# First norm of a two-block transformer step on one core: rows turned unscaled, root applied at copy-out, table loads moved

## Chip, core and metric

The kernel runs on one core of one Trainium2 chip, as one program. The metric is the device time of one execution in microseconds (us). TensorE is called PE in rows of the profile, VectorE DVE, ScalarE ACT, GpSimd POOL, and SyncE SP (it only issues DMAs). SPq and ACTq are the DMA-issuing instructions of SyncE and ScalarE.

## What is computed

Two blocks follow each other on x, 256 tokens of 2048 values, all in fp32. Only the first stage of the first block matters here:

```python
xn = rms_norm(h, pre_mix_norm[i])   # x * rsqrt(mean(x*x) + eps) * gain
proj = xn @ w_in[i]                 # 2048 x 4608
```

Then come head norms with rotary angles on the first heads (gains `q_norm`, `k_norm`), a neighbourhood attention with a relative position bias and a global attention, `w_o`, an MLP, a gate, and the second block with its own projections, conv, scan and MLP. Nine further norms and all other weights are untouched by the change.

The root is one number per token, the gain one number per channel. With r a token's root, (r x g) W = r ((x g) W): the root can be applied to the product's rows.

## The kernel before

**Tiling.** Tokens lie on partitions in two halves (TH = 2 of 128). Each weight matrix is streamed once, in pieces of 512 KB: 256 rows (two times 128, `raw[:, slot, 2, 512]`) by 512 columns. Eight pieces are a chunk of 512 output columns; w_in has nine chunks, pieces 0 to 71. NSLOT = 4 pieces are held.

**Split arithmetic.** A piece lands in `raw` (SyncE, `load`, L507). ScalarE writes `whi`, its value in the matmul's reduced format (`split`, L595); VectorE writes the remainder `wlo = raw - whi` (L1492). TensorE multiplies hi by hi, hi by lo and lo by hi for both token halves and both 128-row blocks, 12 matmuls of 128x512 a piece (L1075), into two PSUM banks per chunk, pairs of banks in turn. The stationary side is `xhi` and `xlo`, the transposed activations, in 16 blocks kt of 128 channels.

**What orders the stream.** Piece p is loaded when `lo_done` has reached p - 3, so when its slot's `raw` has been split. ScalarE splits piece p when it has landed and TensorE has finished piece p - 4. TensorE's `chunk` waits for `lo_done`. ScalarE and VectorE run three pieces ahead of TensorE in program order: in `chunk(p)`, step u splits piece p + 3 + u, and what stands in `extra` goes ahead of that split. A chunk's copy-out (`evac_to`, L611) comes after its eight steps.

**The norm.** `norm("norm0")` on ScalarE squares token half 0 (L619) and VectorE half 1 (L1507); VectorE forms the mean (L1510), GpSimd the power -0.5 (L2004), and then each scales one half into `xs` (L621, L1515). TensorE turns `xs` in eight groups of four 128x128 transposes into two PSUM banks in turn (`turn`, L1050); ScalarE copies a group out with the gain as `xhi` (L626), VectorE makes `xlo` (L1521). `first_chunk` puts groups 0 to 3 before piece 0 and groups 4 to 7 between pieces 0, 1 and 2.

**What is loaded at the start.** SyncE's queue: the identity (`small`), fifteen loads of small vectors as rows of 128 values into `vecs` (L499), the rope tables and column mask (`early`, L501), then the weight pieces. ScalarE's queue: x (`res`, L636), the bias table copied 64 times within memory (`bias_rows`, L637), and `gqk`, where q_norm (512 bytes) is copied to 128 partitions times 8 heads (L638) and k_norm to 128 times 2 (L640). TensorE turns all vectors into columns in one go (L1100) and VectorE copies them into `cols` (L1540); norm0's gain and 15 others lie there. The columns of c_2 get an exp at the start (L645) and the rest of their silu only before `postnorm("post0")`.

**Bias.** `bias_load` (L524) gathers 32 loads of 64 KB from `bias_rows` into `bm`, two after each piece of chunks 1 and 2. When all are in, GpSimd adds the column mask to `bm` in one instruction (L2015), and only then serves the head rotations that VectorE starts with chunk 4's splits.

Of the kernel before, what the change touches and what calls it, by code (L numbers as in the profile page):

```python
# [7 lines left out]
ALU = mybir.AluOpType  # L8
# [6 lines left out]
P = 128  # L15
T = 256
# [24 lines left out]
    [("pre_mix_norm", 16), ("pre_mlp_norm", 16), ("pre_ple_norm", 16), ("norm_pre_mix_2", 16),  # L41
# [74 lines left out]
def build(nc, I, out):  # L116

    ctx = ExitStack()
    with ctx:
# [64 lines left out]
        vecs = at("vecs", [P, len(VEC_GROUPS), P], F32, work_at + 48 * K)  # L184
# [97 lines left out]
        x_in = sem("x_in")  # L282
# [203 lines left out]
        def _(sp):  # L486
            sp.dma_start(small[:], I["k_small"]).then_inc(small_in, 16)
            for gi, group in enumerate(VEC_GROUPS):
                r = 0
                for name, rows in group:  # L490
                    if name == "conv_dw_w_2a":
                        src = I["conv_dw_w_2"][0].rearrange("a (b p) -> (a b) p", p=P)[0:128]
                    elif name == "conv_dw_w_2b":
                        src = I["conv_dw_w_2"][0].rearrange("a (b p) -> (a b) p", p=P)[128:248]
                    elif name == "c_ctx_2":
                        src = I[name].rearrange("(b p) -> b p", p=P)
                    else:
                        src = I[name][0].rearrange("(b p) -> b p", p=P)
                    sp.dma_start(vecs[r:r + rows, gi, :], src).then_inc(vec_in, 16)  # L499
                    r += rows  # L500
            sp.dma_start(early[:], I["k_early"]).then_inc(early_in, 16)  # L501
# [85 lines left out]
        def _(act):  # L587
# [42 lines left out]
            def postnorm(k, row, wait_row, gain):  # L630
# [5 lines left out]
            act.dma_start(res[:], rows_of(I["x"][0])).then_inc(x_in, 16)  # L636
            act.dma_start(bias_rows, bass.AP(I["rel_pos_bias"].tensor, 0, [[0, GRID], [1, NB]])).then_inc(bias_copied, 16)  # L637
            act.dma_start(gqk[:, 0:A_Q * HD].rearrange("p (h d) -> p h d", d=HD),  # L638
                          bass.AP(I["q_norm"].tensor, 0, [[0, P], [0, A_Q], [1, HD]])).then_inc(gqk_in, 16)
            act.dma_start(gqk[:, A_Q * HD:].rearrange("p (h d) -> p h d", d=HD),  # L640
                          bass.AP(I["k_norm"].tensor, 0, [[0, P], [0, A_KV], [1, HD]])).then_inc(gqk_in, 16)
            for u in range(3):
                split(u, u)
            act.wait_ge(vec_cols, 1)
            nc.scalar.activation(stat[:, 64:96], cols[:, COL["c_2"]:COL["c_2"] + 32], ACT.Exp, scale=-1.0).then_inc(c_exp, 1)  # L645
            norm("norm0", res, lambda e: e.wait_ge(x_in, 16), col("pre_mix_norm"))
            p0, g0 = plan["in"]
            with act.Fori(0, 4) as i:
                for c in range(2):
                    chunk(i * 16 + (8 * c + p0), evac_to(proj, i * (2 * NCH) + c * NCH, g0 + c))  # L650
            chunk(p0 + 64, evac_to(proj, 8 * NCH, g0 + 8))
# [392 lines left out]
        def _(pe):  # L1044
# [50 lines left out]
            pe.wait_ge(small_in, 16)  # L1095
            pe.wait_ge(vec_in, 16 * sum(len(g) for g in VEC_GROUPS))
            c = 0
            for gi, group in enumerate(VEC_GROUPS):
                rows = sum(n for _, n in group)
                ins = nc.tensor.transpose(ps[:, MB, c:c + rows], vecs[0:rows, gi, :], ident[0:rows, 0:rows])  # L1100
                c += rows
            ins.then_inc(vec_turned, 1)

            p0, g0 = plan["in"]
            pe.wait_ge(S["xs", "norm0"], 2)
            first_chunk(p0, g0, lambda n: norm_turn("norm0", n), 8, t_free, TG["norm0"][0])
            with pe.Fori(0, 4) as i:
                for c in (1, 2):
                    chunk(i * 16 + (8 * c + p0), i * 2 + (g0 + c), xhi, xlo, par=g0 + c)
# [368 lines left out]
        def _(dve):  # L1478
# [58 lines left out]
            for u in range(3):  # L1537
                split(u, u)
            dve.wait_ge(vec_turned, 1)
            nc.vector.tensor_copy(cols[:], ps[:, MB]).then_inc(vec_cols, 1)  # L1540
            norm("norm0", res, lambda e: e.wait_ge(x_in, 16), col("pre_mix_norm"))
# [45 lines left out]
            for c in range(IN1 // NCH):  # L1587
                chunk(p0 + 8 * c, extra=rotate(c - 4) if 4 <= c < 8 else {})
# [46 lines left out]
            dve.wait_ge(c_exp, 1)  # L1635
            cc, ce = cols[:, COL["c_2"]:COL["c_2"] + 32], stat[:, 64:96]
            step(nc.vector.tensor_scalar(ce, ce, 1.0, None, ALU.add))
            step(nc.vector.reciprocal(ce, ce))
            nc.vector.tensor_tensor(ce, ce, cc, ALU.mult).then_inc(silu_done, 1)
            dve.wait_ge(silu_done, 1)  # L1640

# [473 lines left out]
```

## Time and profile before

| | us |
|---|---|
| median of 3 runs | 3124.39 (3123.58 to 3125.54) |
| profiled execution, its own time | 3127.27 |
| its span in the trace | 3125.5 |
| PE busy | 2863.6 (92%) |
| DVE busy | 2080.2 (67%) |
| ACT busy | 1338.3 (43%) |
| POOL busy | 210.7 (7%) |

The profiled execution lies 2.9 us above the median. A busy share is a mean over stages with different limits. "Idle before" in a row, in square brackets, is how long the engine stood before the instruction and what ended it. PEclk is the granted TensorE clock, 1.00 being 2.4 GHz. The DMA share is that of 16 engines. Matmuls are pipelined and their ends modelled, so that rows of neighbours overlap.

### The profile page before, as it was taken

What the parts mean: (1) busy time and instruction counts of PE and PEld (TensorE: products, weight loads), DVE (VectorE), ACT (ScalarE), POOL (GpSimd) and SP (SyncE); (2) the same over time, 40 slices, a digit from 0 to 9 for tenths busy, and PEclk for the clock granted to TensorE, in tenths of its full rate; (3) what the DMA queues carried; (4) which work ended last, traced back from release to release, by engine and by line L of the source; (5) the groups of instructions that cost most, each with busy time, mean ns of one, the idle gap of its engine ahead of it and who ended that gap; (6) DMA issues with size and microseconds to landing.
All of it is one profiled execution on the core that took longest, in us unless ns stands there. A gap on an engine that the chain in (4) does not pass through costs nothing.

```text
span 3125.5 us, 39386 instructions
## 1 busy us (share of the span) xinstructions
PE 2863.6 (92%) x13257; PEld 2376.2 (76%) x13257; DVE 2080.2 (67%) x2265; ACT 1338.3 (43%) x1571; POOL 210.7 (7%) x116
## 2 busy tenths in 40 slices
PE   4998959999999996959799999999996999999997
PEld 3786848878888885747578888888875888888886
DVE  3565479889897986577658549566646555555555
ACT  3346434344343434433444444564443434344443
POOL 0100011010010101030000000000001101010000
PEclk9999979999999998979899999999997999999998
DMA  6761648888888883645266666512653666666664
GB/s 168 197 195 55 194 149 292 304 289 292 277 296 293 296 299 123 199 148 162 87 219 197 198 186 195 168 55 74 210 188 108 208 213 206 220 199 217 207 207 150
DMA packets 322563, 620.29 MB, mean 198 GB/s; under 512 B 27399, under 2 KB 29575, under 8 KB 320647
## 3 DMA queue, kind: packets, MB, share of 16 engines
q1 hardware_dynamic: 318439, 597.93, 60.4%
q10 hardware_dynamic: 3936, 19.96, 2.0%
q8 instruction: 105, 1.72, 0.2%
q14 instruction: 83, 0.68, 0.1%
HBM read 613.62 MB, written 5.15 MB: 198 GB/s over the span
## 4 chain that ended last, share of the span: by engine, by line
PE 85%; DVE 7%; DMA 2%; issue 2%; ACT 2%; SPq 1%; POOL 1%; DVEq 0%; ACTq 0%; POOLq 0%
PE ps L1075 79%; DMA raw<-w_in 2%; DVE wlo L1492 1%; PE ps L1050 1%; PE ps L1186 1%; PE ps L1196 1%; DVE res L1535 1%; DVE tcol L1739 1%; DVE xs L1532 1%; PE ps L1378 1%; PE ps L1396 1%; PE ps L1358 1%; DVE xlo L1731 0%; POOL res L2008 0%; DVE lg L1772 0%
## 5 line engine op out<-in xcount | busy, mean ns | idle before, releaser
L1492 DVE TENSOR_TENSOR wlo<-raw,whi 128x1024 fp32r<-128x1024 f32 x943 | 1173.4, 1251 | 840.0 <-ACT whi L595 835.8
L595 ACT ACTIVATE whi<-raw 128x1024 fp32r<-128x1024 f32 x943 | 998.6, 1061 | 1378.5 <-PE ps L1075 1260.2
L1075 PE MATMUL ps<-whi,xhi 128*128 128x512 f32 x2656 | 1050.0, 395 | 38.2 <-DVE wlo L1492 20.3
L1075 PE MATMUL ps<-wlo,xhi 128*128 128x512 f32 x2656 | 1041.1, 392 | 0.0
L1075 PE MATMUL ps<-whi,xlo 128*128 128x512 f32 x2656 | 1041.1, 392 | 0.0
L1075 PEld LDWEIGHTS ps<-whi,xhi 128*128 128x128 f32 x2656 | 503.8, 190 | 148.4 <-issue 31.2
L1075 PEld LDWEIGHTS ps<-whi,xlo 128*128 128x128 f32 x2656 | 503.2, 189 | 106.4
L1075 PEld LDWEIGHTS ps<-wlo,xhi 128*128 128x128 f32 x2656 | 504.0, 190 | 102.7
L1075 PE MATMUL ps<-whi,hhi 128*128 128x512 f32 x1040 | 406.7, 391 | 0.0
L1075 PE MATMUL ps<-whi,hlo 128*128 128x512 f32 x1040 | 404.7, 389 | 0.0
L1075 PE MATMUL ps<-wlo,hhi 128*128 128x512 f32 x1040 | 404.6, 389 | 0.0
L1662 DVE SCALAR_TENSOR_TENSOR macc<-mraw,stat,macc 128x512 f32<-128x512 f32 x480 | 354.0, 767 | 4.5
L1075 PEld LDWEIGHTS ps<-whi,hlo 128*128 128x128 f32 x1040 | 195.2, 188 | 40.8
L1075 PEld LDWEIGHTS ps<-whi,hhi 128*128 128x128 f32 x1040 | 195.3, 188 | 39.7
L1075 PEld LDWEIGHTS ps<-wlo,hhi 128*128 128x128 f32 x1040 | 195.3, 188 | 39.6
L2036 POOL TENSOR_TENSOR sqrow<-rrow 128x512 f32<-128x512 f32 x64 | 106.4, 1683 | 1226.9 <-ACT rrow L726 1226.9
L1050 PE MATMUL ps<-small,xs 128*128 128x128 f32 x192 | 39.7, 370 | 138.0 <-ACT xs L759 38.9
L1050 PEld LDWEIGHTS ps<-small,xs 128*128 128x128 f32 x192 | 30.6, 190 | 146.6 <-ACT xs L759 39.5
L726 ACT ACTIVATE rrow<-ps 128x512 f32<-128x512 f32 x64 | 34.8, 596 | 65.0 <-PE ps L1075 65.0
L1679 DVE TENSOR_TENSOR yrow<-ps,yrow 128x512 f32<-128x512 f32 x64 | 41.2, 686 | 25.3 <-PE ps L1075 25.3
L2004 POOL TENSOR_TENSOR stat<-stat 128x2 f32<-128x2 f32 x11 | 7.8, 705 | 743.5 <-DVE stat L1510 743.5
L1819 DVE SCALAR_TENSOR_TENSOR yT<-uT,cols,yT 128x252 f32<-128x252 f32 (+17 forms) x144 | 52.9, 432 | 0.0
(238 smaller groups left out, 1628.2 us busy)
## 6 DMA issues: line engine op xcount, KB each, us to landing
raw<-w_in SPq DMA_DIRECT2D x296, 512.0 KB, 4.3
raw<-mlp_w SPq DMA_DIRECT2D x259, 512.0 KB, 4.4
mraw<-w_mod SPq DMA_DIRECT2D x192, 512.0 KB, 5.4
raw<-w_up SPq DMA_DIRECT2D x128, 512.0 KB, 5.3
raw<-w_down SPq DMA_DIRECT2D x128, 512.0 KB, 5.3
raw<-w_o SPq DMA_DIRECT2D x32, 512.0 KB, 4.5
raw<-w_ple_gate SPq DMA_DIRECT2D x32, 512.0 KB, 4.6
raw<-w_out SPq DMA_DIRECT2D x32, 512.0 KB, 4.6
```

Of the source, the lines that this page charges most:

```text
L595: nc.scalar.activation(whi[:, s % NSLOT], raw[:, s % NSLOT], ACT.Copy).then_inc(hi_done, 1)
L726: ins = nc.scalar.activation(rrow[:, th], ps[:, bank(g0 + j) + th], ACT.Relu)
L1050: ins = nc.tensor.transpose(ps[:, TB[t % 2], c:c + P], src, ident)
L1075: ins = nc.tensor.matmul(ps[:, bank(par) + th], a[:, kt, th * P:(th + 1) * P], b[:, (s + u) % NSLOT, k], start=(kt == 0 and m == 0), stop= ...
L1186: ins = nc.tensor.transpose(ps[:, TB[(t0 + h) % 2], a * T + th * P:a * T + (th + 1) * P], sqrow[:, th, f:f + P], ident)
L1196: ins = nc.tensor.matmul(ps[:, MB, bass.ds(n * 8 + (2 * b + v), 1)], macc[:, v, m % 3, b * P:(b + 1) * P], ones[:, 0:1], start=True, stop= ...
L1358: ins = nc.tensor.matmul(out_of[:, :, 0:4:3] if d == 0 else out_of[:, :, 1:3], w, sums_r[:, m:m + 2].rearrange("p l (r c) -> p l r c", r=2 ...
L1492: nc.vector.tensor_tensor(wlo[:, s % NSLOT], raw[:, s % NSLOT], whi[:, s % NSLOT].bitcast(F32), ALU.subtract)\
L1662: ins = nc.vector.scalar_tensor_tensor(out=a, in0=w, scalar=x, in1=a, op0=ALU.mult, op1=ALU.add)
L1679: ins = nc.vector.tensor_tensor(y, ps[:, bank(g0 + j) + th], y, ALU.add)
L1819: nc.vector.scalar_tensor_tensor(out=y, in0=tap_part(uT[:, ct], ct, dd, True), scalar=wcol(TAPS // 2 + dd, ct), in1=y, op0=ALU.mult, op1=A ...
L2036: nc.gpsimd.tensor_tensor(sqrow[:, th], rrow[:, th], rrow[:, th], ALU.mult).then_inc(sq_done, 1)
```

## The change

- The gain of norm0 is loaded alone, first after the identity, turned and copied to `cols` alone.
- x is loaded in two halves of the channels, with a semaphore each. TensorE turns `res` itself (`x_turn`), groups 0 and 1 before piece 0, group u + 2 ahead of piece u. The copy-outs with the gain (`x_high`, `x_low`) stand between the splits. Nothing is scaled before the product.
- The square sums of x and the mean are computed ahead of the split of piece 9, into scratch (`xjunk`). The copy-out of each of w_in's nine chunks applies the root, as a per-partition scale (`evac_scaled`); ScalarE's loop over chunks is written out.
- The fourteen other vector loads go out after piece 4, their transposes stand before piece 10 and their copy in chunk 1. `early`, `bias_rows` and both `gqk` loads go out after piece 8, all on SyncE's queue. The bias gathers follow the pieces of chunks 2 and 3.
- The silu of the c columns is finished in chunk 3 instead of ahead of post0.

The diff, cut to its core:

```diff
@@ SyncE
+            sp.dma_start(vecs[0:KT, 0, :], I["pre_mix_norm"][0].rearrange("(b p) -> b p", p=P)).then_inc(gain_in, 16)
+            def vector_loads():
+                for gi, group in enumerate(VEC_GROUPS):
...
+            def attention_loads():
+                sp.dma_start(early[:], I["k_early"]).then_inc(early_in, 16)
+                sp.dma_start(bias_rows, bass.AP(I["rel_pos_bias"].tensor, 0, [[0, GRID], [1, NB]])).then_inc(bias_copied, 16)
+                sp.dma_start(gqk[:, 0:A_Q * HD].rearrange("p (h d) -> p h d", d=HD),
+                             bass.AP(I["q_norm"].tensor, 0, [[0, P], [0, A_Q], [1, HD]])).then_inc(gqk_in, 16)
+                sp.dma_start(gqk[:, A_Q * HD:].rearrange("p (h d) -> p h d", d=HD),
+                             bass.AP(I["k_norm"].tensor, 0, [[0, P], [0, A_KV], [1, HD]])).then_inc(gqk_in, 16)
-            chunk(w_in, 0, 0)
-            for c in (1, 2):
-                chunk(w_in, 8 * c, c * NCH, extra={u: (lambda n=16 * (c - 1) + 2 * u: two_biases(n)) for u in range(8)})
-            with sp.Fori(3, IN1 // NCH) as i:
+            chunk(w_in, 0, 0, extra={4: vector_loads})
+            chunk(w_in, 8, NCH, extra={0: attention_loads})
+            for c in (2, 3):
+                chunk(w_in, 8 * c, c * NCH, extra={u: (lambda n=16 * (c - 2) + 2 * u: two_biases(n)) for u in range(8)})
+            with sp.Fori(4, IN1 // NCH) as i:
@@ ScalarE
+            for h in range(2):
+                act.dma_start(res[:, :, h * (D // 2):(h + 1) * (D // 2)],
+                              rows_of(I["x"][0])[:, :, h * (D // 2):(h + 1) * (D // 2)]).then_inc(x_in[h], 16)
+            def x_high(g):
+                t0 = TG["norm0"][0]
+                act.wait_ge(t_done, t0 + g + 1)
+                for j in range(2):
+                    kt = 2 * g + j
+                    ins = nc.scalar.activation(xhi[:, kt], ps[:, TB[(t0 + g) % 2], j * T:(j + 1) * T], ACT.Copy, scale=gain0[:, kt:kt + 1])
+                ins.then_inc(t_hi, 1)
...
+            def evac_scaled(dst, col, g, k):
+                def f():
+                    act.wait_ge(rstd_done, RMS[k] + 1)
+                    for th in range(TH):
+                        ins = nc.scalar.activation(dst[:, th, bass.ds(col, NCH)], ps[:, bank(g) + th], ACT.Copy,
+                                                   scale=stat[:, 8 + th:9 + th])
+                    ins.then_inc(acc_free, 1)
+                return f
+            act.wait_ge(vec_cols, 1)
+            split(0, 0)
+            x_high(0)
+            x_high(1)
+            split(1, 1)
+            x_high(2)
+            split(2, 2)
+            for c in range(IN1 // NCH):
+                chunk(p0 + 8 * c, evac_scaled(proj, c * NCH, g0 + c, "norm0"),
+                      extra={0: {1: lambda: x_high(3), 2: lambda: x_high(4), 3: lambda: x_high(5), 4: lambda: x_high(6),
+                                 5: lambda: x_high(7), 6: x_square}, 2: {0: c_exps}}.get(c, {}))
@@ TensorE
+            def x_turn(g):
+                pe.wait_ge(x_in[g // 4], 16)
+                turn(TG["norm0"][0] + g, [(j * T + th * P, res[:, th, (2 * g + j) * P:(2 * g + j + 1) * P])
+                                          for j in range(2) for th in range(TH)])
+            def x_part(u):
+                if u + 2 < 8:
+                    x_turn(u + 2)
+                pe.wait_ge(t_free, TG["norm0"][0] + u + 1)
+            def other_vectors():
+                pe.wait_ge(vec_in, 16 * sum(len(g) for g in VEC_GROUPS[1:]))
+                pe.wait_ge(vec_cols, 1)
+                turn_vectors(1, len(VEC_GROUPS))
-            pe.wait_ge(S["xs", "norm0"], 2)
-            first_chunk(p0, g0, lambda n: norm_turn("norm0", n), 8, t_free, TG["norm0"][0])
+            turn_vectors(0, 1)
+            x_turn(0)
+            x_turn(1)
+            chunk(p0, g0, xhi, xlo, inserts={u: (lambda u=u: x_part(u)) for u in range(8)})
+            chunk(p0 + 8, g0 + 1, xhi, xlo, inserts={2: other_vectors})
+            chunk(p0 + 16, g0 + 2, xhi, xlo)
@@ VectorE
+            def x_mean_square():
...
+            nc.vector.tensor_copy(cols[:, 0:KT], ps[:, MB, 0:KT]).then_inc(vec_cols, 1)
+            split(0, 0)
+            x_low(0)
+            x_low(1)
+            split(1, 1)
+            x_low(2)
+            split(2, 2)
+            in_extra = {0: {1: lambda: x_low(3), 2: lambda: x_low(4), 3: lambda: x_low(5), 4: lambda: x_low(6), 5: lambda: x_low(7),
+                            6: x_mean_square}, 1: {4: other_columns}, 3: {1: silu_columns}}
```

## Rows read from the trace of the kernel before

**Rows 1.** The page: its span and the chain that ended last, by engine.
```profile
span 3125.5 us, 39386 instructions
...
PE 85%; DVE 7%; DMA 2%; issue 2%; ACT 2%; SPq 1%; POOL 1%; DVEq 0%; ACTq 0%; POOLq 0%
```

**Rows 2.** Timeline of the start: start us, us, engine, line, operation, out<-in, count, [idle before].
```profile
1.24 0.60 ACTq L637 DMA_DIRECT2D bias_rows<-rel_pos_bias  x1
...
2.50 3.06 ACTq L640 DMA_DIRECT2D gqk<-k_norm  x1
...
8.04 0.29 SPq L499 DMA_DIRECT2D vecs<-conv_ln_b  x1
...
24.39 1.27 PE L1100 MATMUL ps<-small,vecs 112*128 112x112 f32 x5 [24.39 <-DMA vecs<-conv_ln_b]
...
28.95 1.06 ACT L595 ACTIVATE whi<-raw 128x1024 fp32r<-128x1024 f32 x1 [22.08 <-DMA raw<-w_in]
...
30.04 3.79 DVE L1492 TENSOR_TENSOR wlo<-raw,whi 128x1024 fp32r<-128x1024 f32 x3 [30.04 <-ACT whi L595]
...
37.73 2.00 ACT L621 ACTIVATE xs<-res,stat 128x2048 f32<-128x2048 f32 x1 [1.15 <-POOL stat L2004]
...
39.79 1.97 PE L1050 MATMUL ps<-small,xs 128*128 128x128 f32 x8 [14.13 <-ACT xs L621]
...
40.94 1.69 ACT L626 ACTIVATE xhi<-ps,cols 128x256 fp32r<-128x256 f32 x4 [1.21 <-PE ps L1050]
...
41.82 1.73 DVE L1521 SCALAR_TENSOR_TENSOR xlo<-ps,cols,xhi 128x256 fp32r<-128x256 f32 x4 [2.80 <-ACT xhi L626]
...
44.43 0.78 PE L1075 MATMUL ps<-whi,xhi 128*128 128x512 f32 x1
...
48.85 1.03 PE L1050 MATMUL ps<-small,xs 128*128 128x128 f32 x8
```

**Rows 3.** DMA issues of the whole execution: issuer, count, size, median us to landing.
```profile
raw<-w_in SPq DMA_DIRECT2D x296, 512.0 KB, 4.3
...
res<-x ACTq DMA_DIRECT2D x1, 2048.0 KB, 8.4
...
bias_rows<-rel_pos_bias ACTq DMA_DIRECT2D x1, 930.0 KB, 10.1
...
gqk<-k_norm ACTq DMA_DIRECT2D x1, 128.0 KB, 25.1
```

**Rows 4.** Windows: start:end, length, busy by engine, PEclk, DMA share, GB/s.
```profile
18.00:19.00 1.00, 0.00 (x0) 0.00 (x0) 0.00 (x0) 0.00 (x0) 0.00 (x0) 1.00 0.88 33
...
27.00:28.00 1.00, 0.00 (x0) 0.00 (x0) 0.00 (x0) 0.00 (x0) 0.00 (x0) 1.00 1.06 409
```

**Rows 5.** DMA queue of ScalarE, 11.3 to 25 us: packets, MB, share of 16 engines.
```profile
q10 hardware_dynamic: 1046, 0.53, 81.9%
```

**Rows 6.** Timeline of ScalarE, copy-outs of chunks 0, 3 and 4.
```profile
71.07 1.09 ACT L611 ACTIVATE proj<-ps 128x512 f32 x2 [0.82 <-PE ps L1075]
...
144.54 1.09 ACT L611 ACTIVATE proj<-ps 128x512 f32 x2 [1.75 <-PE ps L1075]
...
166.30 1.09 ACT L611 ACTIVATE proj<-ps 128x512 f32 x2 [1.75 <-PE ps L1075]
```

**Rows 7.** Timeline of TensorE, first matmuls after two later waits.
```profile
1568.39 0.47 PE L1075 MATMUL ps<-whi,xhi 128*128 128x512 f32 x1 [2.98 <-DVE wlo L1492]
...
2376.92 0.79 PE L1075 MATMUL ps<-whi,xhi 128*128 128x512 f32 x1 [3.95 <-DVE xlo L1731]
```

**Rows 8.** Timeline around the mask addition on GpSimd.
```profile
106.64 8.96 POOL L2015 TENSOR_TENSOR bm<-bm,early 128x4096 f32<-128x4096 f32 x1 [68.94 <-DMA bm<-bias_rows]
...
106.88 13.20 DVE L1492 TENSOR_TENSOR wlo<-raw,whi 128x1024 fp32r<-128x1024 f32 x4 [1.26 <-ACT whi L595]
...
116.73 0.80 PE L1075 MATMUL ps<-whi,xhi 128*128 128x512 f32 x1 [4.99 <-DVE wlo L1492]
```

**Rows 9.** The window behind the wait at 116.73, columns as in rows 4.
```profile
118.00:120.00 2.00, 2.00 (x6) 1.52 (x6) 2.00 (x2) 0.00 (x0) 0.00 (x0) 0.50 0.88 262
```

More of the change, by code:

```diff
@@ L501, in _ @@
-            sp.dma_start(early[:], I["k_early"]).then_inc(early_in, 16)
+            sp.dma_start(vecs[0:KT, 0, :], I["pre_mix_norm"][0].rearrange("(b p) -> b p", p=P)).then_inc(gain_in, 16)
+            def vector_loads():
+                for gi, group in enumerate(VEC_GROUPS):
+                    r = 0
+                    for name, rows in group if gi else ():
+                        if name == "conv_dw_w_2a":
+                            src = I["conv_dw_w_2"][0].rearrange("a (b p) -> (a b) p", p=P)[0:128]
+                        elif name == "conv_dw_w_2b":
+                            src = I["conv_dw_w_2"][0].rearrange("a (b p) -> (a b) p", p=P)[128:248]
+                        elif name == "c_ctx_2":
+                            src = I[name].rearrange("(b p) -> b p", p=P)
+                        else:
+                            src = I[name][0].rearrange("(b p) -> b p", p=P)
+                        sp.dma_start(vecs[r:r + rows, gi, :], src).then_inc(vec_in, 16)
+                        r += rows
@@ L647, in _ @@
[L647 to L651, printed above, removed]
+            for h in range(2):
+                act.dma_start(res[:, :, h * (D // 2):(h + 1) * (D // 2)],
+                              rows_of(I["x"][0])[:, :, h * (D // 2):(h + 1) * (D // 2)]).then_inc(x_in[h], 16)
+            gain0 = col("pre_mix_norm")
@@ L1092, in first_chunk, with turn_vectors @@
                 chunk(p, g, xhi, xlo, inserts={u: (lambda u=u: before(u)) for u in range(8)})
-            pe.wait_ge(small_in, 16)
[L1096 to L1104, printed above, removed]
-            pe.wait_ge(S["xs", "norm0"], 2)
-            first_chunk(p0, g0, lambda n: norm_turn("norm0", n), 8, t_free, TG["norm0"][0])
-            with pe.Fori(0, 4) as i:
-                for c in (1, 2):
+            def turn_vectors(first, last):
+                c = sum(n for group in VEC_GROUPS[:first] for _, n in group)
+                for gi, group in enumerate(VEC_GROUPS[first:last], first):
+                    rows = sum(n for _, n in group)
+                    ins = nc.tensor.transpose(ps[:, MB, c:c + rows], vecs[0:rows, gi, :], ident[0:rows, 0:rows])
+                    c += rows
+                ins.then_inc(vec_turned, 1)
+            def x_turn(g):
[10 more added lines that the diff above has]
+                turn_vectors(1, len(VEC_GROUPS))
+            p0, g0 = plan["in"]
+            pe.wait_ge(small_in, 16)
+            pe.wait_ge(gain_in, 16)
+            turn_vectors(0, 1)
[4 more added lines that the diff above has]
+            chunk(p0 + 16, g0 + 2, xhi, xlo)
+            with pe.Fori(0, 3) as i:
+                for c in (3, 4):
                     chunk(i * 16 + (8 * c + p0), i * 2 + (g0 + c), xhi, xlo, par=g0 + c)
@@ L1535, in postnorm, with x_low @@
                 nc.vector.tensor_tensor(res[:, 1], res[:, 1], xs[:, 1], ALU.add).then_inc(S["res", k], 1)
-            for u in range(3):
-                split(u, u)
-            dve.wait_ge(vec_turned, 1)
-            nc.vector.tensor_copy(cols[:], ps[:, MB]).then_inc(vec_cols, 1)
-            norm("norm0", res, lambda e: e.wait_ge(x_in, 16), col("pre_mix_norm"))
+            gain0, n0 = col("pre_mix_norm"), COL["pre_mix_norm"]
+            def x_low(g):
+                t0, h0 = TG["norm0"]
+                dve.wait_ge(t_hi, h0 + g + 1)
+                for j in range(2):
+                    kt = 2 * g + j
+                    ins = nc.vector.scalar_tensor_tensor(out=xlo[:, kt], in0=ps[:, TB[(t0 + g) % 2], j * T:(j + 1) * T],
+                                                         scalar=gain0[:, kt:kt + 1], in1=xhi[:, kt].bitcast(F32),
+                                                         op0=ALU.mult, op1=ALU.subtract)
+                ins.then_inc(t_free, 1)
@@ new lines, in x_mean_square @@
+            def x_mean_square():
+                dve.wait_ge(x_in[0], 16)
+                dve.wait_ge(x_in[1], 16)
+                nc.vector.tensor_tensor_reduce(out=xjunk[1][:], in0=res[:, 1], in1=res[:, 1], scale=1.0, scalar=0.0,
+                                               op0=ALU.mult, op1=ALU.add, accum_out=stat[:, 1:2]).then_inc(ss_done, 1)
+                dve.wait_ge(ss_done, 2 * RMS["norm0"] + 2)
+                nc.vector.tensor_scalar(stat[:, 4:6], stat[:, 0:2], 1.0 / D, EPS, ALU.mult, ALU.add).then_inc(ms_done, 1)
@@ new lines, in other_columns, with silu_columns @@
+            def other_columns():
+                dve.wait_ge(vec_turned, 2)
+                nc.vector.tensor_copy(cols[:, KT:NCOL], ps[:, MB, KT:NCOL]).then_inc(vec_cols, 1)
+            def silu_columns():
+                dve.wait_ge(c_exp, 1)
+                cc, ce = cols[:, COL["c_2"]:COL["c_2"] + 32], stat[:, 64:96]
+                step(nc.vector.tensor_scalar(ce, ce, 1.0, None, ALU.add))
+                step(nc.vector.reciprocal(ce, ce))
+                nc.vector.tensor_tensor(ce, ce, cc, ALU.mult).then_inc(silu_done, 1)
@@ L1587, in _ @@
             for c in range(IN1 // NCH):
-                chunk(p0 + 8 * c, extra=rotate(c - 4) if 4 <= c < 8 else {})
+                chunk(p0 + 8 * c, extra=rotate(c - 4) if 4 <= c < 8 else in_extra.get(c, {}))
             def score_max(i):
```

46 lines of the change are left out of this document (15 added, 31 removed).

## Prediction

> **What bounds the kernel now.** I read the page first. TensorE carries 85% of the chain that ended last [rows 1], nearly all of it the weight matmuls of line 1075, so anything that lets that stream begin earlier shortens the span one for one, unless it starves later. Nothing in the change touches the bytes or the matmuls of the other stages; the case is decided in the first 125 us. So I read the timeline of the start [rows 2]. The first weight matmul begins at 44.43. Before it stand, in order: the transposes of all vectors, which wait until 24.39 for the last vector; the first weight piece, which ScalarE gets only at 28.95 after 22.08 us without input; the square sums of x, rstd on GpSimd, the scaling of the rows (2.00 us from 37.73); and from 39.79 the transposes of the scaled rows, with copy-out on ScalarE and the rest on VectorE. Then I asked why data for 44 us of waiting are so late, since x itself was issued first and landed after 8.4 us [rows 3]. The one-microsecond windows show the 16 DMA engines busy for 88% of the time at 18 us and moving 33 GB/s, against 409 GB/s at 27 us, when weights flow [rows 4]. What fills them is ScalarE's queue: between 11.3 and 25 us its 1046 packets took 81.9% of the engines [rows 5]. x and the bias rows had landed by then (1.24 + 10.1 = 11.3), so these are the two loads of the attention gains, `gqk`, 1280 copies of 512-byte vectors: 0.819 x 13.7 us x 16 / 1046 = 172 ns a packet, the last landing at 2.50 + 25.1 = 27.6 [rows 2, 3]. The head of the kernel waits on a queue of slow little packets, and then on a serial norm.
>
> **The change, part by part, in the time of the profiled execution.**
>
> *Start of the weight stream.* At the front now stand only the identity, one gain vector, four pieces (2.1 MB) and x in halves (2.1 MB). x whole took 8.4 us with little beside it [rows 3]. Bounds for the moment when both the first half of x and piece 0 are in: not before 1.7 + 4.3 = 6.0, a piece's usual time to landing; not after all 4.3 MB have gone at 409 GB/s, 2 + 10.5 = 12.5. The two queues share the engines, and a half of x plus one piece plus the identity is 1.7 MB, 4.2 us at full rate, with about the same again taken by what is behind them; I take 8.2. The x transposes run under piece 0's cast. Then, from [rows 2]: cast of piece 0 on ScalarE 1.06, its remainder on VectorE, which stands ahead of the x remainder in program order, 1.23 (3.79 for three, less overlap), two x remainders 0.87, one group of four transposes 0.5 (1.03 for eight) and some gaps: first weight matmul at 12.0, bounds 10 to 16.5. Against 44.43 that is **-32.4**. The serial norm, the rstd and the vector transposes are out of that path; the scaling of 2.00 us is gone.
>
> *Chunk 0.* Before: 44.43 to 71.07 [rows 2, 6]. A piece takes (166.30 - 144.54) / 8 = 2.72 us. Piece 0 lasted 48.85 - 44.43 = 4.4, since its first matmul took 0.78 us where one after a short wait takes 0.47 [rows 7]: the engine came out of idleness slow. The rest was the four groups of transposes between pieces, two batches of eight, 1.03 us each, and under 1 us of waiting. After: 8 x 2.72 + 1.7 slow + 5 groups x 0.5 = 26.0, against 26.6: **-0.6**. Each piece has one x copy-out (0.85 on ScalarE, 0.87 on VectorE) beside its cast (1.06) and remainder (1.23): 1.9 and 2.1 us of 2.72, hidden. The square sums, one pass over 2048 columns on either engine like the 2.00 us at 37.73, sit ahead of the split of piece 9, with the engines three pieces ahead of TensorE: hidden. So is the root at copy-out: a scale from a column, as at 40.94, in the two instructions that are there already. Chunk 0 would end at 38.0.
>
> *Vector loads.* Fourteen issues between piece 4's and piece 5's load. In the trace SyncE had issued the identity and all fifteen by 8.04 + 0.29 = 8.33 [rows 2]; less the start and two issues of 0.4 that is 6.7 us of SyncE. Piece 4's load waits for the remainder of piece 0, about 10.5; piece 5 is issued near 17.5 and landed by 21.5. TensorE wants it at 29. Hidden. Their transposes cost TensorE four instructions in piece 10, **+0.6**, the copy on VectorE 0.6, hidden.
>
> *Attention loads: the new wait.* Early tables, bias rows and gqk now stand in SyncE's own queue, behind piece 8 and ahead of piece 9. I take a queue to be served in order, which no row of before tests, so that piece 9 lands behind all of them. Piece 8 is issued when piece 4's remainder is done, after TensorE has left piece 0: 16.4 + 2.4 = 18.8. Pieces 5 to 8 are then moving until about 24 (2.1 MB at 409 GB/s from 18.8). Then 0.3 MB of tables 0.7, the bias rows' 0.93 MB 2.3, gqk, piece 9's 1.3 and 0.9 for its completion; ScalarE and VectorE 2.35. gqk: 1046 packets cost 11.2 us of all engines in [rows 5], and 1280 at 172 ns are 13.8; from the bias rows' landing to k_norm's it is 16.3, with SyncE's packets in it. From below, at the weights' rate, it is 1.6. The nearest row is ScalarE's own share, 11.2 to 13.8 us; I take 11.7, near its measured part, since the two windows' edges cut packets. Piece 9 is ready at 24 + 0.7 + 2.3 + 11.7 + 2.2 + 2.35 = 43.3. TensorE wants it at 38.0 + 2.72 = 40.7. **+2.6** of waiting. Lower bound 0 (and then nothing); upper bound 16.3 in place of 11.7, so 7.2. Between lies a step: after a wait of 2.98 the next matmul still took 0.47, after 3.95 it took 0.79 [rows 7], and a wait of 4.99 before piece 23 was followed by a granted clock of 0.50, so 1.2 GHz, and six matmuls in 2 us [rows 8, 9]. Chunks 1 to 3 together lasted 144.54 - 71.07 = 73.5 [rows 6], 8.2 more than three times 21.76, of which 5.0 is that wait: the slow matmuls cost about 3. So from about 3.5 us on a wait here costs 3 more. What else queues behind these four issues on SyncE: pieces 9 to 12, which come in 1.3 us apart against 2.72 for TensorE, so one wait and no more.
>
> *The bias adds.* The 32 small loads move from chunks 1 and 2 to 2 and 3, and with them GpSimd's 8.96 us addition, under which VectorE's four remainders took 13.20 where three took 3.79 before: the 4.99 us wait [rows 2, 8]. It now falls near piece 31, still ahead of the head rotations. Same price: 0, give or take 1.
>
> *The silu columns* leave the way to post0, where VectorE was waiting for TensorE anyway: 0.
>
> Sum: -32.4 - 0.6 + 0.6 + 2.6 = -29.8. Span 3125.5 - 29.8 = 3095.7; the profiled execution took 3127.27, 2.9 above the median of 3124.39, so on the median **3094.6 us**.
>
> The Trainium skill (DMA: Bandwidth & Descriptors, Specifications) gives 512 bytes as enough for line rate. By that rule the gqk copies would be cheap, 1.5 us at the page's 435 GB/s; [rows 5] disagree, at 172 ns for a packet of that size. The same page (Queues, rings and completion order) says that each DMA engine alternates between queues and takes one queue's descriptors in order; that speaks against putting the tables ahead of piece 9, where before they only shared the engines with the weights, and no row of before has them in one queue.
>
> **Rivals.** (a) *Cheap tables.* The packets were slow because two queues of tiny packets disturbed each other (the vectors ran beside them), and alone on one queue they run near the weights' rate. For it: the 512-byte vectors and gqk were in flight together, and so it is untried. Against it: SyncE's packets were few, and the engines were ScalarE's for 81.9% of the time. Then piece 9 is on time: -32.4, 3092.0. (b) *Long wait.* gqk takes 14 to 16.3 us, or the bias rows more than 2.3, so that piece 9 waits over 3.5 us; TensorE falls to its lower clock: wait 4.5 to 7, plus 3, so -32.4 + 7.5 to 10 = -25 to -22.4; 3100.7. (c) *Late first data.* x and piece 0 come as late as 12.5. The start is 4.5 later, but piece 9 hangs on the queue and not on TensorE, so its wait shrinks by the same until it is gone; net +2 to +3: 3097. (d) *The other side: the weight stream halted.* SyncE's issues stall behind gqk (its second copy took ScalarE's queue 3 us to issue) and the packets, all on one queue, cost several times 172 ns. The change turns slower from a wait at piece 9 of 32.4 - 3 = 29.4 us: gqk would need 11.7 + 29.4 - 2.6 = 38.5 us, 480 ns a packet, nearly three times the row. At 550 ns it is +5.5, 3130.
>
> **Chances.** Forecast 0.47, (a) 0.17, (b) 0.22, (c) 0.11, (d) 0.02, and 0.01 that a moved wait eats it all. The range 3090 to 3102 takes in the first four, with the start's early bound (-2) below and (b)'s mildest half above. 0.2% is 6 us, about what this kernel's measurement can tell from no change: faster 0.97, same 0.01, slower 0.02.
>
> **What would show it.** First weight matmul at 10 to 14 us; chunk 0's copy-out near 38; a TensorE wait of 1 to 4 us before piece 9 whose releaser is the remainder of a late weight load, with DMA windows of high share and some 50 GB/s from 27 to 39; no wait for pieces 5 to 8; the GpSimd addition with a 5 us wait near piece 31; from piece 40 on the traces run parallel, shifted by 29 to 30 us. I am wrong if the low-rate windows are short (a), if matmuls of 0.63 us follow piece 8 (b), or if TensorE waits for a piece between 5 and 8, which the vector loads would answer for.

## Result and profile after

The changed kernel takes 3096.98 us (median of 4, 3093.81 to 3100.11) against 3124.71; the ratio is 0.991 with a 95% interval of 0.9898 to 0.9922. The forecast was 3094.6. The profiled execution took 3099.24 with a span of 3097.4, so 28.1 less span than before.

The page of the changed kernel, its span and the chain by engine (answers to rows 1):

```profile
span 3097.4 us, 39317 instructions
...
PE 88%; DVE 6%; DMA 2%; ACT 2%; issue 1%; POOL 1%; ACTq 0%; DVEq 0%; SPq 0%; POOLq 0%
```

The timeline of its start, with columns as in rows 2:

```profile
6.88 1.97 PE L1092 MATMUL ps<-small,res 128*128 128x128 f32 x8
...
10.39 1.28 ACT L609 ACT_TABLE_LOAD   x1 [10.39 <-DMA raw<-w_in]
11.68 1.06 ACT L609 ACTIVATE whi<-raw 128x1024 fp32r<-128x1024 f32 x1
...
15.67 0.78 PE L1117 MATMUL ps<-whi,xhi 128*128 128x512 f32 x1
...
49.77 0.80 PE L1117 MATMUL ps<-whi,xhi 128*128 128x512 f32 x1 [4.66 <-DVE wlo L1554]
```

The first weight matmul stands at 15.67, not 44.43. Transposes of x run from 6.88, right behind that of the gain, which waited until 6.69 for its load, but ScalarE has nothing to cast until 10.39; then comes the load of its activation table, 1.28 us, and only then the cast. TensorE then runs to piece 9 and waits 4.66 us for it.

The copy-outs of chunks 2 to 4 (answers to rows 6), and what surrounds GpSimd's mask addition (rows 8):

```profile
94.00 1.27 ACT L677 ACTIVATE proj<-ps,stat 128x512 f32<-128x512 f32 x2 [1.60 <-PE ps L1117]
...
119.98 1.27 ACT L677 ACTIVATE proj<-ps,stat 128x512 f32<-128x512 f32 x2 [1.62 <-PE ps L1117]
...
141.74 1.27 ACT L677 ACTIVATE proj<-ps,stat 128x512 f32<-128x512 f32 x2 [1.60 <-PE ps L1117]
```

```profile
102.41 9.04 POOL L2109 TENSOR_TENSOR bm<-bm,early 128x4096 f32<-128x4096 f32 x1 [61.88 <-DMA bm<-bias_rows]
...
103.31 12.63 DVE L1554 TENSOR_TENSOR wlo<-raw,whi 128x1024 fp32r<-128x1024 f32 x4 [1.49 <-ACT whi L609]
...
112.59 0.67 PE L1117 MATMUL ps<-whi,xhi 128*128 128x512 f32 x1 [2.31 <-DVE wlo L1554]
```

The window behind that wait (answer to rows 9), its last three columns being the granted clock, the share of the DMA engines and GB/s:

```profile
114.00:116.00 2.00, 2.00 (x6) 1.57 (x5) 1.94 (x2) 0.00 (x0) 0.00 (x0) 0.50 0.87 280
```

VectorE's remainder, 12.63 us for four pieces, again runs while GpSimd adds the mask. TensorE waits 2.31 us for it and then works at a granted clock of 0.50 (1.2 GHz).

Chunk 4's copy-out, the last point before the stages that the change does not touch, moved from 166.30 to 141.74, by 24.6 us. The other 3.5 us of span fell in later stages.

There, in the MLP of the second block, the kernel before waits at three turns of the loop; the changed kernel waits at none of them. TensorE's matmuls behind these turns in the kernel before:

```profile
2559.96 0.49 PE L1075 MATMUL ps<-whi,xhi 128*128 128x512 f32 x1 [1.53 <-DVE yrow L1679]
...
2740.59 0.49 PE L1075 MATMUL ps<-whi,xhi 128*128 128x512 f32 x1 [1.73 <-DVE yrow L1679]
...
2921.05 0.49 PE L1075 MATMUL ps<-whi,xhi 128*128 128x512 f32 x1 [1.55 <-DVE yrow L1679]
```

What held piece 9: one-microsecond windows, columns as in rows 4:

```profile
33.00:34.00 1.00, 1.00 (x9) 0.83 (x7) 1.00 (x1) 0.00 (x0) 0.00 (x0) 1.00 0.14 44
...
45.00:46.00 1.00, 0.11 (x1) 0.00 (x0) 0.00 (x0) 0.00 (x0) 0.00 (x0) 1.00 1.05 399
```

SyncE's queue between 32 and 43 us (packets, MB, share of 16 engines):

```profile
q1 hardware_dynamic: 803, 0.41, 12.5%
```

The two gqk issues, with KB and us to landing:

```profile
gqk<-q_norm SPq DMA_DIRECT2D x1, 512.0 KB, 18.7
...
gqk<-k_norm SPq DMA_DIRECT2D x1, 128.0 KB, 19.4
```

From 31 to 44 us next to nothing but gqk moves, at some 40 GB/s, as forecast; but in this profile the DMA engines are busy for 14% and not for 88%. That share differs between executions that move the packets at the same rate. The same burst in the second profile of the changed kernel (32 to 42 us), with the table load early (32 to 41) and with the loads moved alone (46 to 57), all three runs described below:

```profile
q1 hardware_dynamic: 767, 0.40, 43.0%
...
q1 hardware_dynamic: 731, 0.38, 82.7%
...
q1 hardware_dynamic: 818, 0.42, 76.7%
```

That is 73 packets a microsecond at a share of 12.5%, and 77, 81 and 74 at 43.0, 82.7 and 76.7%. The duration of a packet in the profile (rows 5, 172 ns) was therefore no measure of what the load costs or of what the engines could still have done. What sets the share stays open.

### The profile page after: what moved, and what is told of

The parts are those of the page before. It is cut to its first block, busy times and chain, and to the rows that moved or that the text cites. A ratio compares the mean times of both kernels' runs of the same rounds, so it can differ in the third digit from the quotient of the medians.

```text
span 3097.4 us, 39317 instructions
## 1 busy us (share of the span) xinstructions
PE 2860.0 (92%) x13258; PEld 2374.2 (77%) x13258; DVE 2078.0 (67%) x2265; ACT 1337.1 (43%) x1570; POOL 210.8 (7%) x116
## 4 chain that ended last, share of the span: by engine, by line
PE 88%; DVE 6%; DMA 2%; ACT 2%; issue 1%; POOL 1%; ACTq 0%; DVEq 0%; SPq 0%; POOLq 0%
PE ps L1117 81%; PE ps L1092 1%; DMA raw<-w_in 1%; PE ps L1248 1%; PE ps L1258 1%; DVE wlo L1554 1%; DVE res L1597 1%; DVE tcol L1833 1%; DVE xs L1594 1%; PE ps L1420 1%; PE ps L1440 1%; PE ps L1458 0%; DVE xlo L1825 0%; POOL res L2102 0%; DVE lg L1866 0%
```

## Experiments

As a measure free of the later stages I use the copy-out of chunk 4 in each kernel's profile. Times are medians with their spread; the kernel before took 3117.5 to 3130.4 in 31 executions beside these runs.

**The kernel before once more.** Unaltered, one execution.

> The kernel before once more, unaltered, for a second profile: by my reading its start repeats within 1 us (first weight matmul 44.4, wait of 5.0 us under the mask addition, chunk 4's copy-out 166.3) and differences in its time come from the loops behind.

It took 3122.43 us.

```profile
42.95 0.78 PE L1075 MATMUL ps<-whi,xhi 128*128 128x512 f32 x1
...
112.16 0.50 PE L1075 MATMUL ps<-whi,xhi 128*128 128x512 f32 x1 [2.56 <-DVE wlo L1492]
...
160.47 1.08 ACT L611 ACTIVATE proj<-ps 128x512 f32 x2 [1.75 <-PE ps L1075]
```

The expectation fell. The first weight matmul comes 1.5 us earlier and the wait under the mask addition is 2.56, not 4.99; chunk 4 leaves at 160.47, 5.8 us before the first profile's 166.30. The stretch up to chunk 4 differs by that much between two executions of this kernel.

**The changed kernel once more.** Unaltered.

> The changed kernel once more, unaltered. Theory: its start is the same in every execution (first weight matmul 15.7, a wait of 4 to 5 us before piece 9, copy-out of chunk 4 at 139 to 142), and its four times between 3093.8 and 3100.1 differ by the MLP loops, where nothing was changed, and by whether the clock falls under the mask addition. Median 3095 to 3099.

Measured 3097.13 (3095.0 to 3104.48), ratio 0.9914 (0.99 to 0.9927).

```profile
48.74 0.50 PE L1117 MATMUL ps<-whi,xhi 128*128 128x512 f32 x1 [4.50 <-DVE wlo L1554]
...
110.78 0.80 PE L1117 MATMUL ps<-whi,xhi 128*128 128x512 f32 x1 [2.23 <-DVE wlo L1554]
...
139.86 1.27 ACT L677 ACTIVATE proj<-ps,stat 128x512 f32<-128x512 f32 x2 [1.60 <-PE ps L1117]
```

The waits repeat: 4.50 before piece 9, 2.23 under the mask addition. So of the 28 us between the medians, the stretch up to chunk 4 explains 18.7 to 26.4, depending on which two profiles are paired (160.47 or 166.30 less 139.86 or 141.74).

The three waits in the second MLP repeat too. They add up to 4.8, 4.9 and 5.0 us in the two profiles of the kernel before and in that of the run with the bias gathers moved alone, and the ten other profiles show no wait of TensorE there, which all have the changed kernel's loads or its unscaled rows or both. So these 5 us go with the changed program. By what, no run here shows: the stage's work is the same.

**The loads moved alone.** The norm as before, in the changed kernel:

```diff
-            x_turn(0)
-            x_turn(1)
-            chunk(p0, g0, xhi, xlo, inserts={u: (lambda u=u: x_part(u)) for u in range(8)})
+            pe.wait_ge(S["xs", "norm0"], 2)
+            first_chunk(p0, g0, lambda n: norm_turn("norm0", n), 8, t_free, TG["norm0"][0])
...
-                chunk(p0 + 8 * c, evac_scaled(proj, c * NCH, g0 + c, "norm0"),
+                chunk(p0 + 8 * c, evac_to(proj, c * NCH, g0 + c), extra={2: {0: c_exps}}.get(c, {}))
```

> The changed kernel with the norm as it was before (square sums, root, scaled rows, then the transposes; plain copy-out), all loads where the change puts them. My theory: the two halves of the change are not additive, since piece 9 hangs on the queue of tables and not on TensorE. The first weight matmul comes some 9 us later than in the changed kernel (about 25 us instead of 15.7), but the wait of 4.66 us before piece 9 and the slow matmuls behind it (3 us) go, so the time is only 1 to 4 us above the changed kernel's, 3098 to 3102. Rival, the parts add up: the whole 9 us show, about 3106.

Measured 3114.52 (3108.55 to 3117.11), ratio 0.997 (0.9957 to 0.9982).

```profile
25.41 0.78 PE L1112 MATMUL ps<-whi,xhi 128*128 128x512 f32 x1
...
34.94 3.92 ACT L609 ACTIVATE whi<-raw 128x1024 fp32r<-128x1024 f32 x4
...
63.70 0.79 PE L1112 MATMUL ps<-whi,xhi 128*128 128x512 f32 x1 [9.72 <-DVE wlo L1548]
...
155.61 1.08 ACT L625 ACTIVATE proj<-ps 128x512 f32<-128x512 f32 x2 [1.60 <-PE ps L1112]
```

Both expectations missed. The first matmul came as said, at 25.41, but the wait before piece 9 did not go; it grew to 9.72, and chunk 4 leaves 13.9 us later than in the changed kernel. Here ScalarE casts pieces 3 to 6 only behind all eight x copy-outs, at 34.94. Piece 8's load, and the tables behind it, go out when piece 4 is split, at 38.8 (24.9 in the changed kernel): 13.4 us behind the first matmul instead of 9.2. The burst of tables is tied to the progress of the splits, not to a time of its own.

**The unscaled rows alone.** Loads in their old places, in the changed kernel:

```diff
-            chunk(w_in, 0, 0, extra={4: vector_loads})
-            chunk(w_in, 8, NCH, extra={0: attention_loads})
+            vector_loads()
+            sp.dma_start(early[:], I["k_early"]).then_inc(early_in, 16)
+            chunk(w_in, 0, 0)
+            chunk(w_in, 8, NCH)
```

with `bias_rows` and `gqk` issued by ScalarE behind x.

> The changed kernel with all vector and table loads in their old places ahead of the weights and in ScalarE's queue behind x; only the transposes from the tokens and the root at copy-out stay (the gathers of the bias stay in chunks 2 and 3). My theory: TensorE then starts when piece 0 is in, near 29 us, plus 5 us: first weight matmul at 34, 10 us earlier than before, no wait before piece 9, and the shorter wait under the mask addition: 3109 to 3115. Rival, that the norm chain was what held the start: first weight matmul near 16 to 20 and a time near the changed kernel's.

Measured 3109.29 (3102.37 to 3110.3), ratio 0.9955 (0.9938 to 0.9972).

```profile
32.78 0.78 PE L1116 MATMUL ps<-whi,xhi 128*128 128x512 f32 x1
...
148.93 1.27 ACT L676 ACTIVATE proj<-ps,stat 128x512 f32<-128x512 f32 x2 [1.60 <-PE ps L1116]
```

As expected: TensorE starts when piece 0 is in and cast. In medians the parts are worth 9 and 14 us, and together 28. At the first weight matmul they nearly add up: 19.0 and 11.7 us against 28.8 for both (from 44.43). Behind that, the loads alone lose 9.72 us and slow matmuls at piece 9, the changed kernel 4.66 and slow matmuls, and this run nothing; and each median holds the 5 us of the second MLP, which the two parts together bring only once. How the 28 divide is not settled more closely than that: profiles of one kernel differ by up to 5.8 us at chunk 4.

**Is it the packets or their source?** gqk read from 1280 different rows of x; the gains of q and k are wrong then, the work is the same.

```diff
-bass.AP(I["q_norm"].tensor, 0, [[0, P], [0, A_Q], [1, HD]])
+bass.AP(I["x"].tensor, 0, [[D, P], [2 * HD, A_Q], [1, HD]])
-bass.AP(I["k_norm"].tensor, 0, [[0, P], [0, A_KV], [1, HD]])
+bass.AP(I["x"].tensor, HD, [[D, P], [2 * HD, A_KV], [1, HD]])
```

> The changed kernel with the two gqk loads reading 1280 different pieces of 512 bytes (out of x) instead of the same 512 bytes 1280 times; the gains of q and k are therefore wrong in the output, the work is the same. Theory A, the repeated source address is what costs: the loads take 2 us instead of 13, piece 9 is in time, no wait and no slow matmuls: 7 to 8 us below the changed kernel, about 3088. Theory B, the number of 512-byte packets costs: the same 13 us, the same 4.66 us wait, the same time.

Measured 3093.13 (3087.23 to 3093.8), ratio 0.9896 (0.9879 to 0.9912). The gqk issues, as above, and chunk 4's copy-out:

```profile
gqk<-x SPq DMA_DIRECT2D x1, 512.0 KB, 7.8
gqk<-x SPq DMA_DIRECT2D x1, 128.0 KB, 8.5
```

```profile
134.40 1.27 ACT L677 ACTIVATE proj<-ps,stat 128x512 f32<-128x512 f32 x2 [1.60 <-PE ps L1117]
```

Theory A stands for the loads, the wait and chunk 4: the same number of packets of the same size lands after 7.8 us instead of 18.7, with nothing else changed; no wait before piece 9; chunk 4 leaves 7.3 us earlier. The median fell by 3.9 us and not by 7 to 8; its four executions lie at 3093.80 or below, the nine of the changed kernel at 3093.81 or above. What is slow is the repeated reading of the same 512 bytes. It is not slow throughout: in the changed kernel the queue moved 935 packets between 31 and 44 us, some 72 a microsecond, and in the next microsecond 331:

```profile
q1 hardware_dynamic: 331, 0.26, 76.8%
```

By the order of issue k_norm's 256 copies, also of one vector, were in that quick end. Why they pass quickly stays open.

**Is it the order within the queue?** The four table loads issued by ScalarE, behind its copy-out of group 4:

```diff
-            chunk(w_in, 8, NCH, extra={0: attention_loads})
+            chunk(w_in, 8, NCH)
...
-                      extra={0: {1: lambda: x_high(3), 2: lambda: x_high(4),
+                      extra={0: {1: lambda: x_high(3), 2: lambda: (x_high(4), attention_loads()),
```

> The changed kernel with the early tables, the bias rows and gqk issued by ScalarE in its own queue, at about the same moment (behind the fourth split). Theory A, order within one queue holds piece 9 back: the weights pass the tables in the other queue and the wait before piece 9 goes: 7 us below the changed kernel. Theory B, gqk holds up the DMA engines whichever queue it is in, as at the start of the kernel before, where engines were busy for 88% at 33 GB/s: pieces 8 to 11 crawl beside it, the wait before piece 9 stays or grows to 5 to 10 us.

Measured 3098.44 (3093.04 to 3101.82), ratio 0.9923 (0.9906 to 0.9939). Between 34 and 42 us the two queues (ScalarE's is q10) and the weights issued in that stretch; then TensorE's timeline with the wait:

```profile
q10 hardware_dynamic: 633, 0.32, 12.7%
q1 hardware_dynamic: 3, 0.01, 0.2%
...
raw<-w_in SPq DMA_DIRECT2D x3, 512.0 KB, 14.8
```

```profile
49.91 0.79 PE L1117 MATMUL ps<-whi,xhi 128*128 128x512 f32 x1 [6.11 <-DVE wlo L1554]
```

Theory B stands. Pieces were waiting in SyncE's queue, and in 8 us it moved three packets while ScalarE's moved 633; a piece took 14.8 us to land. Chunk 4 leaves at 141.95, as in the changed kernel. So gqk holds up the other queue too, and my reason for piece 9's wait, that it stands behind gqk in one queue, was too narrow: it waited in either.

**The repeated reads taken away.** Gains loaded once per partition, widened by ScalarE in chunk 2:

```diff
+                sp.dma_start(gqk[:, 0:HD], bass.AP(I["q_norm"].tensor, 0, [[0, P], [1, HD]])).then_inc(gqk_in, 16)
+                sp.dma_start(gqk[:, A_Q * HD:(A_Q + 1) * HD], bass.AP(I["k_norm"].tensor, 0, [[0, P], [1, HD]])).then_inc(gqk_in, 16)
...
+                for a, n in ((0, A_Q - 1), (A_Q, A_KV - 1)):
+                    ins = nc.scalar.activation(gqk[:, (a + 1) * HD:(a + 1 + n) * HD].rearrange("p (h d) -> p h d", d=HD),
+                                               gqk[:, a * HD:(a + 1) * HD].unsqueeze(1).to_broadcast([P, n, HD]), ACT.Copy)
```

> The changed kernel with q_norm and k_norm loaded once per partition (256 packets instead of 1280) and copied to the eight and two heads by ScalarE in chunk 2. If the repeated source address sets a price per packet (13 us for 1280), the two loads take 2.6 us, piece 9 is in time, and the copy-out of chunk 4 comes 7.3 us earlier than in the changed kernel, as with the other rows as source: 134.4 instead of 141.7. Rival, a fixed hold-up of any such load: the wait stays above 3 us. Median 7 us below the changed kernel's, near 3090.

Measured 3091.18 (3088.04 to 3094.54), ratio 0.9889 (0.9867 to 0.9911); both loads (64 KB each) land within 7.4 us, there is no wait before piece 9, and chunk 4 leaves at 132.01. The median is 5.8 to 6.0 us below the changed kernel's (3096.98 and 3097.13), of 7 expected. Piece 9's wait and the hold on the queue go with the repeated copies, not with the gains.

**The activation table.** One wait moved:

```diff
-            act.wait_ge(vec_cols, 1)
             split(0, 0)
+            act.wait_ge(vec_cols, 1)
             x_high(0)
```

> The changed kernel with ScalarE's wait for the gain column moved behind its first cast, and nothing else. In the changed kernel the load of the activation table (1.28 us) stands behind two waits and begins at 10.39, when piece 0 is in. Theory: with the wait moved it is done at once at the start, and the first weight matmul comes 1.3 us earlier, 14.4. Whether this shows at chunk 4's copy-out tells if the wait before piece 9 hangs on TensorE's progress (then 1.3 us earlier, 140.4) or on the table loads alone (then unchanged, 141.7).

One execution, 3095.01 us.

```profile
1.76 1.28 ACT L609 ACT_TABLE_LOAD   x1 [1.76 <-issue]
...
14.17 0.78 PE L1117 MATMUL ps<-whi,xhi 128*128 128x512 f32 x1
...
47.12 0.79 PE L1117 MATMUL ps<-whi,xhi 128*128 128x512 f32 x1 [4.78 <-DVE wlo L1554]
```

The start moves by 1.5 us and the wait stays (4.78): matmuls, splits and table burst move together. Chunk 4 leaves at 137.29, which is 4.5 and 2.6 us earlier than in the two profiles of the changed kernel; the start explains 1.5, and in this one execution the clock stayed at 1.00 behind the wait under the mask addition (2.85). Forecasting a start delay as shortening the wait, as my rival (c) did, was wrong.

**Bias gathers moved alone**, in the kernel before:

```diff
-            for c in (1, 2):
-                chunk(w_in, 8 * c, c * NCH, extra={u: (lambda n=16 * (c - 1) + 2 * u: two_biases(n)) for u in range(8)})
+            chunk(w_in, 8, NCH)
+            for c in (2, 3):
+                chunk(w_in, 8 * c, c * NCH, extra={u: (lambda n=16 * (c - 2) + 2 * u: two_biases(n)) for u in range(8)})
```

> The kernel before with one part of the change: the 32 bias gathers follow the pieces of chunks 2 and 3 instead of 1 and 2. In the kernel before the wait of TensorE under GpSimd's mask addition is 4.99 us, in the changed kernel 2.31. Theory A, VectorE's lead: with the gathers right behind the late start the loads land every 2.84 us and the lead shrinks; a chunk later it is full, so the wait falls to about 2.3 here too and chunk 4's copy-out comes 3 to 4 us earlier than 166.3. Theory B, the shorter wait comes from the early start alone: 166.3 stays.

Measured 3123.22 (3120.49 to 3127.45, 10 executions), ratio 0.9999 (0.9989 to 1.0009). Its profile shows what theory A said, a wait of 2.1 and chunk 4 at 161.34; but the unaltered kernel's second profile shows the same (2.56 and 160.47), and the time did not move. The edit is worth nothing that shows; the 4.99 of rows 8 was one draw out of a scatter.

**Three edits together**: gains widened, table early, and both halves of x in SyncE's queue behind pieces 0 and 1.

> The changed kernel with three edits: gains widened on ScalarE, table load early, and both halves of x in SyncE's queue, behind pieces 0 and 1, so that piece 0 has the DMA engines alone. Expected: piece 0 in by about 5 us instead of 10.4, first half of x by 7.5, first weight matmul near 11 instead of 15.7, no wait before piece 9, chunk 4's copy-out near 130; time 11 to 12 us below the changed kernel, near 3085. Rival: vector and table loads then meet pieces 5 to 9 earlier and a wait before one of them takes back several us.

Measured 3088.44 (3079.99 to 3093.83), ratio 0.9887 (0.9865 to 0.991). Piece 0's cast begins at 5.80, the first matmul at 12.21 (x's first half now comes later, 8.4), chunk 4 leaves at 127.77, 14.0 us before the changed kernel; no rival wait appeared. The median shows 8.5 of it, its four times spread over 14 us.

**The mask addition cut in four**, on top of these:

```diff
+            for n in range(4):
+                b4 = b3[:, n * part:(n + 1) * part]
+                nc.gpsimd.tensor_tensor(b4, b4, colmask.unsqueeze(1).to_broadcast([P, part, GRID]), ALU.add)\
+                    .then_inc(bias_done, 1)
```

> The kernel of the three edits (gains widened on ScalarE, table load early, x in SyncE's queue) with GpSimd's mask addition cut in four instructions of 2.3 us. Theory: VectorE's remainders slip in between them, TensorE does not wait any more (1.6 us in the three-edit kernel, 2.3 to 2.9 in others), chunk 4's copy-out near 126 instead of 127.8; time 2 us below the three-edit kernel at most. Rival, VectorE stays locked out over all four: no difference.

Measured 3082.89 (3079.62 to 3088.43), ratio 0.9862 (0.9847 to 0.9877), the lowest median of the study. Its four times overlap with those of the three edits (3079.99 to 3093.83), so the time does not show what the cut is worth; chunk 4 leaves 2.1 us earlier, as expected.

```profile
90.60 12.48 POOL L2118 TENSOR_TENSOR bm<-bm,early 128x1024 f32<-128x1024 f32 x4 [53.80 <-DMA bm<-bias_rows]
...
125.70 1.27 ACT L683 ACTIVATE proj<-ps,stat 128x512 f32<-128x512 f32 x2 [1.60 <-PE ps L1123]
```

GpSimd's four parts take 12.48 us instead of 9.04, VectorE's remainders take some 3.2 us each (four in 12.68 us), and TensorE does not wait. In the changed kernel one remainder, which takes 1.23 us elsewhere, lasts from 103.31 to about 112 us, so as long as the whole addition: what is cut is the time for which a single remainder stands still.

## Why the prediction held, point by point

The time and the range held; the terms did not all, and by its own signs the prediction did less well than by its number. No piece between 5 and 8 was waited for, piece 9 was, and behind a late load. But the first matmul came at 15.67 and not by 14; the copy-out of chunk 0 at 50.85 and not near 38, since in ScalarE's program it stands behind the casts of pieces 9 and 10; the wait was 4.66 and not 4 at most; the addition's wait 2.31 and not 5; the shift from chunk 4 on 24.6 and not 29 to 30; and the matmuls of 0.63 us that were to speak for rival (b) followed piece 8. Rival (b) had 3100.7.

- **Start of the stream**: forecast 12.0, measured 15.67, a gain of 28.8 and not 32.4. Two misses: piece 0 was castable at 10.39 where I took 8.2, with x's queue holding 60.3% of the engines in the first 8 us and the other, with the weights, 17.6%, and the activation table, 1.28 us, which I left out: in the kernel before it had loaded at 5.59, far ahead of the first cast. The steps from the cast on, 4.0 us, were right within 0.2.
- **Chunk 0 and piece 8**: forecast 28.7 from the first matmul to the wish for piece 9, measured 29.4 (45.11 - 15.67). Copy-outs, square sums, vector loads and the root at copy-out were all hidden, as said.
- **The wait at piece 9**: right in place and cause, mis-sized. Forecast 2.6, measured 4.66 and 4.50. Forecast were a low-rate stretch from 27.0 to 38.7, piece 9 in at 40.9 and ready at 43.3; it ran from 31 to 44, piece 9 was in at 47.40 and ready at 49.72. The stretch began 4 us late, since piece 8 went out at about 24.5 and not at 18.8; gqk took 13 us where I took 11.7 out of an interval of 11.2 to 16.3; and from its end to the landing it took 3.4 us where I took 2.2, of which 0.9 stood on no row. TensorE's wish for piece 9 was late by 4.4 us, which hid most of this. So the case that occurred was rival (b), with its clock penalty: the window below shows a granted clock of 0.50 (1.2 GHz) behind it, and chunk 1's copy-out at 72.24 is 2.8 us later than 49.77 + 7 x 2.72 + 0.6.

```profile
50.00:52.00 2.00, 2.00 (x5) 1.59 (x6) 1.03 (x1) 2.00 (x4) 0.00 (x0) 0.50 0.68 156
```

- **Queue order** was taken as the mechanism; the run with two queues shows that it is not needed: the weights are held up in another queue as well. The Trainium skill (DMA: Bandwidth & Descriptors, Queues, rings and completion order) has each engine alternate between queues at packet boundaries. By that rule the weights in the other queue should have passed; in that run 3 packets of them did beside 633. The Trainium skill's same page (Specifications), by which 512 bytes are enough for line rate, I set aside for the 172 ns of rows 5; gqk from different rows (7.8 us to land) shows that the size was not the cause, and from one address (18.7 us) the rule does not hold. And the 172 ns themselves were one execution's: packets went at the same rate at a share of 12.5%. Rival (a) had the cause wrong as well: the packets are as slow alone (72 a microsecond) as in company (1046 in 13.7 us, 76).
- **The mask addition**: forecast unchanged, measured 2.31 against 4.99, chunk 3 lasting 25.98, so 4.2 us too long, where the first profile's chunks 1 to 3 were 8.2 too long together. The second profile of the kernel before has the shorter wait too (2.56, and 4.5 us too long together); no gain of the change, but 4.0 us that the comparison with the first profile puts to its credit.
- **The step in the clock penalty**: I put it at 3.5 us of waiting. Under the mask addition, waits of 2.11 (bias gathers moved alone), 2.31 (changed kernel) and 2.37 (loads moved alone) were followed by a granted clock of 0.50, while after 2.33 (unscaled rows alone), 2.36 (gains widened) and 2.85 (table load early) it stayed at 1.00. Waits of 2 to 3 us are uncertain.
- **Sum**: 24.6 us at chunk 4 against a forecast of 29.8. The start gave 3.6 less, chunk 0 and piece 8 took 0.7 more, the wait 2.1 and the slow matmuls behind it 2.8, together 9.2; the shorter wait under the mask addition gave 4.0 back. The 3.5 us in later stages bring the span to 28.1. No term stood for them. Span less chunk 4's copy-out was 2959.2 and 2960.1 in the two profiles of the kernel before, 2955.7 and 2955.4 in those of the changed one, and between 2949.2 and 2960.9 over all kernels: waits of 1.3 to 3.0 us where the first block's MLP loop turns come and go from one profile to the next, while the three waits of the second block's MLP, 4.8 us, stand in every profile of a kernel without the changed program and in none with it. Whatever in the program does it, the forecast did not know of it. So the good fit of the total is in part luck: the first 166 us gave 5 us less than I summed, 9 less without the draw under the mask addition (160.47 less 139.86 is 20.6), and the stages behind them 3 to 5 more.

## What to carry to other kernels

A vector that is broadcast by DMA to many places should be read once per partition and widened on chip; here the many reads of one small vector held up the other queue as well, and neither the packet count nor the busy share of the DMA engines told what they cost. A load that nobody wants for 60 us still has a price when it stands among loads that are wanted now: ask how long it holds the queue and how many pieces are ahead. And before a wait of one profile is put into a sum, look at a second profile of the same kernel.

## What the runs showed of the hardware

- Copies of one 512-byte vector to many places moved at 71 to 81 packets a microsecond, some 40 GB/s, in nine profiles, while the share of the DMA engines read anything from 12.5% to 91.5%. 1280 packets of the same size from different addresses landed after 7.8 us instead of 18.7. The 64 copies of the 14.9 KB bias table, also from one address, went with the rest: between 25 and 31 us the queue moved 2.3 MB at 326 to 421 GB/s, so that the table took some 2.4 us (an estimate).
- They hold up other queues: three weight pieces beside them took 14.8 us to land (median) instead of the 4.5 of seven later pieces in the kernel with the gains widened.
- x with 4 KB rows in one queue beside weights with 2 KB rows in the other: in the first 8 us x's queue moved 1.74 MB and the other, identity and gain included, 0.44 MB (rows below). The first piece took 8.7 us to land, against 4.1 when it went ahead of x.
- ScalarE's table load came behind a separate wait that stood ahead of the first cast (10.39), and at 1.76 with that wait moved behind the cast.
- A granted clock of 0.50 (1.2 GHz) followed some of TensorE's waits of 2.1 to 2.6 us; after others of 2.33 to 2.98 us it stayed at 1.00.
- One VectorE remainder of 1.23 us lasted about 9 us under a GpSimd addition of 9.04 us; with the addition in four parts, four remainders took 3.2 us each.

```profile
q10 hardware_dynamic: 442, 1.74, 60.3%
q1 hardware_dynamic: 321, 0.44, 17.6%
```
